# A two-block transformer on one core: another order of a mixer unit's steps on ScalarE and VectorE, squares added in twos, and the last gate's columns summed at another place

## The chip, the cores and the metric

The kernel runs on one core of one Trainium2 chip. The metric is the device time of one execution in microseconds, the median over several runs. The kernel before takes 1094.76 us (three runs, 1092.68 to 1098.1). One more execution was taken with the hardware profiler; it took 1096.54 us, of which 1094.6 us lie between its first and its last instruction (the span). All durations below are of that execution.

## The reference

A residual stream x of 256 tokens by 1024 features goes through three layers, all in float32. Each layer has a mixer (projection, attention, output projection) and a feed-forward part, and each part is normed on the way in; in the first two layers also on the way out. Scale, shift and gate of every part are a vector times a matrix. Cut to what matters:

```python
def first_block(x, c, ...):                       # two layers
    for layer in range(2):
        shift, scale, gate = split(c @ mod_w[layer, 0] + mod_b[layer, 0])
        h = rms_norm(x, norm_w[layer, 0, 0]) * (1.0 + scale) + shift
        y = mixer_ab(h, ...) if layer == 0 else mixer_cd(h, ...)
        x = x + gate * rms_norm(y, norm_w[layer, 0, 1])
        shift, scale, gate = split(c @ mod_w[layer, 1] + mod_b[layer, 1])
        h = rms_norm(x, norm_w[layer, 1, 0]) * (1.0 + scale) + shift
        y = swiglu(h, ffn_w_in[layer], ffn_w_out[layer])
        x = x + gate * rms_norm(y, norm_w[layer, 1, 1])
def mixer_cd(h, ...):    # softmax heads, and heads with stick-breaking weights
    o_c = moba_attention(...)
    o_d = stick_breaking_attention(...)
    return concatenate([o_c, o_d]) @ w_out
def second_block(x, c_2, ...):                    # one layer
    sh1, sc1, gt1, sh2, sc2, gt2 = split(silu(c_2) @ w_ada + b_ada, 6)
    h = rmsnorm(x, g_norm1) * (1.0 + sc1) + sh1
    q, k, v, z = split(h @ w_in)                  # q, k normed per head and rotated
    attn = block_attention(q, k, v)
    tok = chunked_token_mlp(z, g_tok_v, w_s, b_s)
    x = x + gt1 * (concatenate([rmsnorm(attn), rmsnorm(tok)]) @ w_out)
    h = rmsnorm(x, g_norm2) * (1.0 + sc2) + sh2
    x = x + gt2 * conv_glu_ffn(h, w_up, w_conv, b_conv, w_down)
    return rmsnorm(x, g_final)
```

## The kernel before, in words

Features lie on the 128 partitions, tokens along the free dimension. The weights come as 270 units of 128x1024 floats through a ring of six slots (`raw`, loaded by SyncE). To multiply in float32 with the fast format, each unit is split: ScalarE writes the high part `wH` (L785), VectorE the low part `wL` = raw - `wH` (L1200), and TensorE does three matmuls for each 128x128 piece: high by high, high by low, low by high (L1841 to L1843). A unit is eight pieces, so 24 matmuls; the activations are split the same way into `hH` and `hL`. An engine waits on semaphores and works strictly in the order in which its instructions are written.

The phases follow one another: the first mixer (called ab), feed-forward f0, mixer cd, feed-forward f1, mixer sb (the second block), feed-forward f2, the last norm. In a feed-forward phase a step is three units (gate, up, down).

A mixer phase cd or sb starts with projection units e = 0 to 17 (cd) or 0 to 13 (sb). For each unit, TensorE's `project` fills a bank of PSUM; ScalarE's `unit_column` copies the bank's column 256 into `ucol` (L863; it carries the shift); VectorE's `take_unit` multiplies the bank by `rstd` (L1325, L1327); ScalarE's `finish_unit` adds the column (L870; in sb the square of q and k, L1107, comes first). Beside this, ScalarE splits one later unit at the top of each pass of the loop (`split_upto(base + e + 5)`), and so does VectorE. VectorE also runs `jobs`: 128x1024 products (L602, L604) that build the columns of scale, shift and gate of later parts in `acc0`, `acc1` and `late_acc`. For the units that hold values, TensorE turns the finished unit (`turn_values`, L1920), and VectorE copies it (`values`, L1337). From unit 6 on, TensorE's project of unit e waits until VectorE has taken unit e - 2. Then come the heads, and after them eight output units (`y_unit`).

In sb some more steps lie between the units: after unit 5 ScalarE makes six activations for the norms of q and k (L1116, L1117); VectorE scales q and k at e = 7 and rotates them at e = 9 (L1745 to L1747); TensorE's first scores (`block_scores`, L2385) wait for that and for the finish of unit 10. Behind the heads TensorE sums the columns `modA5` (L1869) and turns the attention output when VectorE has scaled it (L1805, L2461).

The norms: A0 to A6 of x, B0 to B3 of a part's output y, in the order A0, B0, A1, B1, and so on; A6 is the last. ScalarE squares four blocks of 128x512 (L805), TensorE multiplies each block's two halves of 256 columns by a matrix of ones into one sum in bank 6 (L1855, L1856: eight matmuls for a norm), ScalarE makes `rstd` from it (L795, L796). VectorE waits for `rstd` and updates x (L1286, L1297), x is split again (L832, L1265), and TensorE starts the next phase. Between the sums and that start it makes a gate's columns (`mod_sum`, 8 columns) and six spare products (`keep_clock`, L1981).

At the end of f2, TensorE does down(20), then `mod_sum("modG5")` (the last gate), then down(21). VectorE takes the gate, adds the gated output to x (L1311, eight instructions) while ScalarE squares x block by block, and the last norm's eight products (L1275) end the kernel. ScalarE's split of the unit for down(21) is the last of its step, behind `aH` (L935).

## Time and profile before

| | |
|---|---|
| time, median of 3 runs | 1094.76 us |
| the profiled execution: time, span | 1096.54 us, 1094.6 us |
| TensorE (PE) busy | 1036.2 us, 95% |
| VectorE (DVE) busy | 789.8 us, 72% |
| ScalarE (ACT) busy | 557.4 us, 51% |
| mean granted TensorE clock | 0.963 of full speed |
| chain that ended last | PE 75%, DVE 11%, ACT 7%, issue 4%, DMA 3% |
| moved by DMA | 227.60 MB, mean 208 GB/s |

How to read it: busy is the time in which an engine had an instruction in work. The chain is followed back from the last instruction, at each step to what released it, so its shares tell which engine set the time at each moment. The phases in time: cd's units run from about 399 to 462 us, its heads to 502, its output units to 531; sb's units from about 746 to 812, its heads to 854, its output units from 861 on; f2 ends at about 1084. In a row of the timeline stand the start, the duration, engine, line, operation, written and read tile, shape, and in brackets the idle time before it and what ended that.

### The profile page before, as it was taken

What the parts mean: (1) busy time and instruction counts of PE and PEld (TensorE: products, weight loads), DVE (VectorE), ACT (ScalarE), POOL (GpSimd) and SP (SyncE); (2) the same over time, 40 slices, a digit from 0 to 9 for tenths busy, and PEclk for the clock granted to TensorE, in tenths of its full rate; (3) what the DMA queues carried; (4) which work ended last, traced back from release to release, by engine and by line L of the source; (5) the groups of instructions that cost most, each with busy time, mean ns of one, the idle gap of its engine ahead of it and who ended that gap; (6) DMA issues with size and microseconds to landing.
All of it is one profiled execution on the core that took longest, in us unless ns stands there. A gap on an engine that the chain in (4) does not pass through costs nothing.

```text
span 1094.6 us, 21376 instructions
## 1 busy us (share of the span) xinstructions
PE 1036.2 (95%) x8164; PEld 990.6 (90%) x8164; DVE 789.8 (72%) x1288; ACT 557.4 (51%) x1116; POOL 4.6 (0%) x14
## 2 busy tenths in 40 slices
PE   6998879999999999999999999999779999999997
PEld 5997659999999989889899999998767999999996
DVE  4757775788888757768688888765584557787775
ACT  2445663544444454454554444454551366766663
POOL 0100000000000000000000000000000000000000
PEclk9999899999999999979999999999885999999999
DMA  9966666388787647703558888753530134555441
GB/s 361 329 212 219 229 220 244 123 321 301 291 300 291 255 140 246 269 21 112 177 215 320 307 292 305 289 215 131 193 116 1 39 137 154 181 208 186 173 138 56
DMA packets 62409, 227.60 MB, mean 208 GB/s; under 512 B 7010, under 2 KB 7266, under 8 KB 61956
## 3 DMA queue, kind: packets, MB, share of 16 engines
q1 hardware_dynamic: 61556, 224.02, 57.0%
q0 software_dynamic: 640, 2.10, 0.8%
q8 instruction: 48, 0.79, 0.3%
q10 hardware_dynamic: 144, 0.52, 0.1%
q14 instruction: 21, 0.17, 0.0%
HBM read 225.04 MB, written 1.57 MB: 207 GB/s over the span
## 4 chain that ended last, share of the span: by engine, by line
PE 75%; DVE 11%; ACT 7%; issue 4%; DMA 3%; SPq 1%; DVEq 0%; ACTq 0%
PE bank L1841 20%; PE bank L1842 20%; PE bank L1843 20%; ACT wH L785 3%; DMA modbuf<-in_mod_w 3%; DVE acc L604 2%; DVE wL L1200 2%; PE bank L1856 2%; PE bank L1855 2%; PE bank L1869 1%; PE bank L2451 1%; PE bank L1950 1%; DVE otok L1286 1%; PE bank L1981 1%; PE bank L2385 1%
## 5 line engine op out<-in xcount | busy, mean ns | idle before, releaser
L1841 PE MATMUL bank<-hH,wH 128*128 128x258 f32 (+1 forms) x1544 | 448.7, 291 | 10.9 <-DVE hL L1265 7.7
L1842 PE MATMUL bank<-hL,wH 128*128 128x258 f32 (+1 forms) x1544 | 440.8, 286 | 0.0
L1843 PE MATMUL bank<-hH,wL 128*128 128x258 f32 (+1 forms) x1544 | 439.1, 284 | 0.0
L1200 DVE TENSOR_TENSOR wL<-raw,wH 128x1024 fp32r<-128x1024 f32 x270 | 328.1, 1221 | 66.6 <-ACT wH L785 66.4
L1841 PEld LDWEIGHTS bank<-hH,wH 128*128 128x128 f32 x1544 | 295.5, 191 | 20.6 <-issue 13.6
L1843 PEld LDWEIGHTS bank<-hH,wL 128*128 128x128 f32 x1544 | 296.6, 192 | 0.0
L1842 PEld LDWEIGHTS bank<-hL,wH 128*128 128x128 f32 x1544 | 296.1, 192 | 0.5
L785 ACT ACTIVATE wH<-raw 128x1024 fp32r<-128x1024 f32 x270 | 275.5, 1046 | 38.1 <-DMA raw<-in_weights 19.6
L1841 PE MATMUL bank<-aH,wH 128*128 128x256 f32 x592 | 168.6, 285 | 1.2 <-DVE wL L1200 1.2
L1843 PE MATMUL bank<-aH,wL 128*128 128x256 f32 x592 | 168.0, 284 | 0.0
L1842 PE MATMUL bank<-aL,wH 128*128 128x256 f32 x592 | 168.0, 284 | 0.0
L1841 PEld LDWEIGHTS bank<-aH,wH 128*128 128x128 f32 x592 | 113.9, 192 | 2.2 <-DVE wL L1200 1.4
L1842 PEld LDWEIGHTS bank<-aL,wH 128*128 128x128 f32 x592 | 114.0, 193 | 0.0
L1843 PEld LDWEIGHTS bank<-aH,wL 128*128 128x128 f32 x592 | 113.9, 192 | 0.0
L903 ACT ACTIVATE fcol<-bank 128x1 f32<-128x1 f32 x132 | 15.2, 166 | 136.0 <-PE bank L1843 135.9
L1414 DVE TENSOR_TENSOR sn<-bank,rstd 128x256 f32<-128x256 f32 x44 | 18.7, 424 | 51.2 <-ACT fcol L903 51.1
L935 ACT ACTIVATE aH<-sn 128x256 fp32r<-128x256 f32 x66 | 27.5, 417 | 49.4 <-PE bank L1843 24.9
L604 DVE SCALAR_TENSOR_TENSOR acc<-modbuf,par,acc 128x1024 f32<-128x1024 f32 x28 | 35.8, 1280 | 10.3 <-DMA modbuf<-in_mod_w 9.6
L1434 DVE SCALAR_TENSOR_TENSOR pr<-sq,par,pr 128x255 f32<-128x255 f32 x44 | 19.3, 481 | 29.9 <-ACT pr L921 29.9
L908 ACT ACTIVATE sn<-sn,fcol 128x256 f32<-128x256 f32 x44 | 22.4, 510 | 28.3 <-DVE sn L1414 28.3
L917 ACT ACTIVATE sq<-sq,fcol 128x256 f32<-128x256 f32 x44 | 20.1, 503 | 21.0 <-DVE sq L1425 21.0
L1286 DVE TENSOR_TENSOR otok<-bank,rstd 128x512 f32<-128x512 f32 x16 | 10.6, 685 | 25.7 <-ACT rstd L796 25.7
(324 smaller groups left out, 1212.5 us busy)
## 6 DMA issues: line engine op xcount, KB each, us to landing
raw<-in_weights SPq DMA_DIRECT2D x270, 512.0 KB, 4.5
modbuf<-in_mod_w SPq DMA_DIRECT2D x69, 512.0 KB, 6.2
modbuf<-in_w_ada SPq DMA_DIRECT2D x36, 512.0 KB, 6.3
strips<-in_mod_w SPq DMA_DIRECT2D x16, 512.0 KB, 7.2
strips<-in_w_ada SPq DMA_DIRECT2D x12, 512.0 KB, 6.7
strips<-bias_table POOLq DMA_DIRECT2D x8, 256.0 KB, 7.1
otok<-in_cmp_w SPq DMA_DIRECT2D x4, 512.0 KB, 8.4
raw<-in_mod_w SPq DMA_DIRECT2D x2, 512.0 KB, 4.7
```

The lines of the kernel that those rows point to most:

```text
L604: ops.scalar_tensor_tensor(out=dst, in0=src, scalar=cc[:, k:k + 1], in1=dst, op0=ALU.mult, op1=ALU.add).then_inc(mod_used, 1)
L785: nc.scalar.activation(wH[:, slot, :], raw[:, slot, :], ACT.Copy).then_inc(hi_ready[c], 1)
L908: nc.scalar.activation(sn[:, t % 2, 0:S], sn[:, t % 2, 0:S], ACT.Silu, bias=fcol[:, t % 2, 0:1]).then_inc(silu_ready, 1)
L917: last = nc.scalar.activation(z, z, ACT.Identity, bias=fcol[:, t % 2, n:n + 1])
L935: nc.scalar.activation(aH[:, t % 2, :], sn[:, t % 2, S:2 * S], ACT.Copy).then_inc(aH_ready, 1)
L1200: V.tensor_tensor(wL[:, slot, :], raw[:, slot, :], wH[:, slot, :].bitcast(F32), ALU.subtract).then_inc(lo_ready[c], 1)
L1286: chain.inc(V.tensor_tensor(tt[:, 2 * b:2 * b + 2, :], bank[(2 if i == 0 else 0) + b][:, :].rearrange("p (k s) -> p k s", k=2), bcast(rstd ...
L1841: mm(out, lhs_h, rhs_h, start=start, stop=False, skip_group_check=True)
L1842: mm(out, lhs_h, rhs_l, start=False, stop=False, skip_group_check=True)
L1843: return mm(out, lhs_l, rhs_h, start=False, stop=stop, skip_group_check=True)
L1855: mm(bank[6][:, 0:S], ones, buf[:, 0:S], start=(b == 0), stop=False, skip_group_check=True)
L1856: mm(bank[6][:, 0:S], ones, buf[:, S:2 * S], start=False, stop=(b == 3), skip_group_check=True).then_inc(sq_used, 1)
```

## The change

Three edits. First, in both mixers a unit's split moves. ScalarE issues it between `unit_column` and the waits ahead of `finish_unit`, VectorE after `take_unit`; each unit is split in the pass before the one that split it until now, behind that pass's copy of the column. The number of splits stays 270.

On ScalarE in cd, three units in a row. `ucol` is the column, `proj` the unit's tile, `wH` the split. Before:

```order
L785 ACTIVATE wH<-raw 128x1024 [waits unit_used0,raw_full3]
L863 ACTIVATE ucol<-bank 128x1 [waits unit_used2]
L870 ACTIVATE proj<-proj,ucol 128x256 [waits unit_scaled,ucol_ready]
L785 ACTIVATE wH<-raw 128x1024 [waits unit_used1,raw_full4]
L863 ACTIVATE ucol<-bank 128x1 [waits unit_used0]
L870 ACTIVATE proj<-proj,ucol 128x256 [waits unit_scaled,ucol_ready]
```

The same place now:

```order
L874 ACTIVATE proj<-proj,ucol 128x256 [waits unit_scaled,ucol_ready]
L866 ACTIVATE ucol<-bank 128x1 [waits unit_used2]
L788 ACTIVATE wH<-raw 128x1024 [waits unit_used1,raw_full4]
L874 ACTIVATE proj<-proj,ucol 128x256 [waits unit_scaled,ucol_ready]
L866 ACTIVATE ucol<-bank 128x1 [waits unit_used0]
L788 ACTIVATE wH<-raw 128x1024 [waits unit_used2,raw_full5]
```

The split stood behind the finish of a unit, and stands ahead of it now.

On VectorE at the end of cd's units (unit 17, then the first stick-breaking head, L1660 and L1671). `vt` are the values, `strips` a job. Before:

```order
L1200 TENSOR_TENSOR wL<-raw,wH 128x1024 [waits hi_ready0]
L1325 TENSOR_TENSOR sq<-bank,rstd 128x256 [waits v_turned,ucol_ready]
L1337 COPY vt<-bank 128x2x128 [waits v_turned]
L604 SCALAR_TENSOR_TENSOR strips<-modbuf,csil,strips 128x1024 [waits mod_used,job_full2]
L1337 COPY vt<-bank 128x2x128 [waits v_turned,con_landed]
L1660 TENSOR_TENSOR sq<-bank,con 128x384 [waits z_psum]
```

And now:

```order
L1336 TENSOR_TENSOR sq<-bank,rstd 128x256 [waits v_turned,ucol_ready]
L1202 TENSOR_TENSOR wL<-raw,wH 128x1024 [waits hi_ready1]
L1348 COPY vt<-bank 128x2x128 [waits v_turned]
L607 SCALAR_TENSOR_TENSOR strips<-modbuf,csil,strips 128x1024 [waits mod_used,job_full2]
L1348 COPY vt<-bank 128x2x128 [waits v_turned,con_landed]
L1671 TENSOR_TENSOR sq<-bank,con 128x384 [waits z_psum]
```

A further unit's low part stands between taking unit 17 and the first head; it stood behind the last head. In sb it is the same with unit 13.

Second, for the norms B0, B1, B2, B3 and A6 VectorE adds the two halves of each block of squares in place (`add_pair`, four for a norm), and TensorE makes one matmul for a block instead of two. On TensorE, the sums of norm A6 before:

```order
L1855 MATMUL bank<-sq,con 128x256 [waits sq_ready,rstd_ready]
L1856 MATMUL bank<-sq,con 128x256
L1855 MATMUL bank<-sq,con 128x256 [waits sq_ready]
L1856 MATMUL bank<-sq,con 128x256
L1855 MATMUL bank<-pr,con 128x256 [waits sq_ready]
L1856 MATMUL bank<-pr,con 128x256
L1855 MATMUL bank<-pr,con 128x256 [waits sq_ready]
L1856 MATMUL bank<-pr,con 128x256
```

These eight rows are now three, of which the last stands for two matmuls:

```order
L1889 MATMUL bank<-con,strips 128x128 [waits mod_used]
L1889 MATMUL bank<-con,strips 128x128 x7
...
L1870 MATMUL bank<-sq,con 128x256 [waits pair_ready,rstd_ready]
L1870 MATMUL bank<-sq,con 128x256 [waits pair_ready]
L1870 MATMUL bank<-pr,con 128x256 [waits pair_ready] x2
```

The two rows of L1889 ahead of them are the third edit: the eight columns of the last gate, `mod_sum("modG5")`, stand much earlier in TensorE's row, right behind `mod_sum("modA5")` of sb, and write bank 6; they stood between down(20) and down(21) of f2. VectorE takes them with `modA5`'s.

```diff
+        PAIRED = [1, 3, 5, 7, 10]
         def mod_bank(name):
-            return bank[6 if name == "modA1" else 7]
+            return bank[6 if name in ("modA1", "modG5") else 7]
...
+        NUNITS = {"cd": CD_UNITS, "sb": SB_UNITS}
...
                 nc.scalar.activation(ucol[:, e % 2:e % 2 + 1], proj_bank(phase, e)[:, S:S + 1], ACT.Copy,
                                      scale=scale).then_inc(ucol_ready, 1)
+                split_upto(min(BASE[phase] + e + 6, BASE[phase] + NUNITS[phase] + 5))
                 act.wait_ge(ucol_ready, SCALED0[phase] + e + 1)
                 act.wait_ge(unit_scaled, SCALED0[phase] + e + 1)
...
             for e in range(18):
-                split_upto(min(base + e + 5, end + 5))
                 if e == 17:
...
+            def add_pair(n, b):
+
+                buf = squares_buffer(n, b)
+                dve.wait_ge(sq_ready, 4 * n + b + 1)
+                V.tensor_tensor(buf[:, 0:S], buf[:, 0:S], buf[:, S:2 * S], ALU.add).then_inc(pair_ready, 1)
+
             def norm_b(i, m, a, late, base):
 
-                dve.wait_ge(rstd_ready, NORMS.index(f"B{i}") + 1)
+                n = NORMS.index(f"B{i}")
+                for b in range(4):
+                    add_pair(n, b)
+                dve.wait_ge(rstd_ready, n + 1)
...
             for e in range(18):
-                split_upto(min(base + e + 5, end + 5))
                 if e == 16:
                     neg_scores(24, 0)
                 take_unit("cd", e, CD_SCALE[e])
+                split_upto(min(base + e + 6, end + 5))
                 values("cd", e)
                 jobs_upto(cd_jobs(e))
...
-                split_upto(min(base + e + 5, end + 5))
                 take_unit("sb", e)
+                split_upto(min(base + e + 6, end + 5))
                 values("sb", e)
...
             mod_take("modA5")
+            mod_take("modG5")
...
             ffn("f2", 5)
-            mod_take("modG5")
             for b in range(4):
                 residual("f2", 5, b)
+                if b >= 1:
+                    add_pair(NORMS.index("A6"), b - 1)
+            add_pair(NORMS.index("A6"), 3)
             norm_a(6)
...
-                pe.wait_ge(sq_ready, 4 * n + b + 1)
                 buf = squares_buffer(n, b)
+                if n in PAIRED:
+                    pe.wait_ge(pair_ready, 4 * PAIRED.index(n) + b + 1)
+                    mm(bank[6][:, 0:S], ones, buf[:, 0:S], start=(b == 0), stop=(b == 3),
+                       skip_group_check=True).then_inc(sq_used, 1)
+                    return
+                pe.wait_ge(sq_ready, 4 * n + b + 1)
...
-                mod_sum({"f0": "modA2", "f1": "modA4", "f2": "modG5"}[phase])
+                if phase != "f2":
+                    mod_sum({"f0": "modA2", "f1": "modA4"}[phase])
                 down(FT - 1)
...
             mod_sum("modA5")
+            mod_sum("modG5")
             pe.wait_ge(an_out, 2)
```

## Rows read from the trace of the kernel before

**Rows 1.** Waits of TensorE: line, waited for, us in total, times, longest.

```profile
PE bank L1920 <- ACT sq L870: 6.3, 3, 4.4
PE bank L2451 <- DVE pt L1356: 2.8, 1, 2.8
PE bank L2385 <- ACT proj L870: 2.4, 1, 2.4
```

**Rows 2.** Timeline of ScalarE at norm B0: the last two squares.

```profile
183.40 1.33 ACT L805 ACTIVATE pr<-bank 128x512 f32<-128x512 f32 x2
```

**Rows 3.** Timeline of TensorE at norm B0: first and last sum, next phase.

```profile
183.94 0.59 PE L1855 MATMUL bank<-sq,con 128*128 128x256 f32 x2
...
186.96 0.59 PE L1856 MATMUL bank<-pr,con 128*128 128x256 f32 x2
...
192.25 0.36 PE L1841 MATMUL bank<-hH,wH 128*128 128x258 f32 x1 [1.57 <-DVE hL L1265]
```

**Rows 4.** Groups by line: a 128x256 operation of VectorE; busy, mean ns.

```profile
L1454 DVE TENSOR_TENSOR aL<-sn,aH 128x256 fp32r<-128x256 f32 x66 | 27.7, 419 | 1.0 <-ACT aH L935 1.0
```

**Rows 5.** Timeline of ScalarE in cd: one unit, and unit 17's column.

```profile
418.49 1.04 ACT L785 ACTIVATE wH<-raw 128x1024 fp32r<-128x1024 f32 x1
...
421.22 0.51 ACT L870 ACTIVATE proj<-proj,ucol 128x256 f32<-128x256 f32 x1 [1.63 <-DVE proj L1325]
421.63 1.04 ACT L785 ACTIVATE wH<-raw 128x1024 fp32r<-128x1024 f32 x1
...
461.78 0.17 ACT L863 ACTIVATE ucol<-bank 128x1 f32<-128x1 f32 x1
```

**Rows 6.** Timeline of VectorE in cd: a split, and the first head.

```profile
419.56 1.22 DVE L1200 TENSOR_TENSOR wL<-raw,wH 128x1024 fp32r<-128x1024 f32 x1 [0.39 <-ACT wH L785]
...
464.48 0.55 DVE L1660 TENSOR_TENSOR sq<-bank,con 128x384 f32<-128x384 f32 x1
```

**Rows 7.** Timeline of TensorE in cd: two matmuls of unit 2, units 6 and 15.

```profile
409.02 0.28 PE L1842 MATMUL bank<-hL,wH 128*128 128x258 f32 x1
409.14 0.28 PE L1843 MATMUL bank<-hH,wL 128*128 128x258 f32 x1
...
421.18 0.39 PE L1841 MATMUL bank<-hH,wH 128*128 128x258 f32 x1 [0.60 <-DVE proj L1325]
...
450.10 0.44 PE L1920 MATMUL bank<-con,sq 128*128 128x128 f32 x2 [0.57 <-ACT sq L870]
```

**Rows 8.** Busy by stretch, cd's heads, sb's unit 12, sb's heads: engines, then PEclk.

```profile
466.50:480.10 13.60, 13.55 (x53) 11.50 (x53) 8.06 (x24) 5.69 (x16) 0.00 (x0) 0.50 0.01 4
...
801.00:808.00 7.00, 6.80 (x27) 6.00 (x28) 5.95 (x8) 2.51 (x5) 0.00 (x0) 0.51 0.60 184
...
818.20:852.80 34.60, 34.52 (x137) 26.87 (x138) 16.52 (x30) 6.14 (x25) 0.00 (x0) 0.51 0.01 1
```

**Rows 9.** Timeline of ScalarE in sb: after the norms of q and k, unit 6.

```profile
776.87 1.04 ACT L785 ACTIVATE wH<-raw 128x1024 fp32r<-128x1024 f32 x1
...
779.58 1.28 ACT L870 ACT_TABLE_LOAD   x1 [1.61 <-DVE sq L1325]
780.87 0.51 ACT L870 ACTIVATE sq<-sq,ucol 128x256 f32<-128x256 f32 x1
```

**Rows 10.** Timeline of TensorE behind sb's heads.

```profile
854.31 5.58 PE L1869 MATMUL bank<-con,acc 128*128 128x128 f32 x48
860.96 1.10 PE L2461 MATMUL bank<-con,otok 128*128 128x128 f32 x8 [1.07 <-DVE otok L1805]
```

**Rows 11.** Timeline of TensorE at the end of f2.

```profile
1078.07 1.95 PE L1869 MATMUL bank<-con,strips 128*128 128x128 f32 x16
1081.20 0.39 PE L1841 MATMUL bank<-aH,wH 128*128 128x256 f32 x1 [1.17 <-DVE wL L1200]
...
1087.19 0.59 PE L1856 MATMUL bank<-pr,con 128*128 128x256 f32 x2
```

**Rows 12.** Timeline of ScalarE at the end: the last square.

```profile
1085.54 0.63 ACT L805 ACTIVATE pr<-x 128x512 f32<-128x512 f32 x1
```

9 lines of the change are left out of this document (5 added, 4 removed).

## The prediction

> **What bounds the kernel now.** I read in this order: busy shares, TensorE's waits, then the timelines of three engines wherever TensorE stands still. TensorE is busy 95% of the span, so a gain has to come from fewer TensorE instructions on the path, from its idle time, or from stretches at the lower clock. The reader is to see four places.
>
> At norm B0 TensorE runs eight sums without a break; the last of them starts at 186.96, although ScalarE's last square had ended at 183.40 + 1.33 = 184.73 [rows 2, 3]. ScalarE and VectorE wait for these sums, and TensorE waits for them in turn: its next phase starts at 192.25 after 1.57 us idle [rows 3]. The eight matmuls are the path.
>
> In cd a ring bounds the units. ScalarE starts a high part at 418.49, VectorE its low part at 419.56 (1.14 us at its own pace), takes the unit behind it, ScalarE finishes that unit at 421.22 and starts the next high part at 421.63 [rows 5, 6]. That is 3.14 us for a unit. TensorE's matmuls start 0.12 us apart, so a unit of 24 needs 2.89 [rows 7]. TensorE falls behind by 0.25 a unit.
>
> In sb the waits are few and long: 4.4 us for the finish of unit 6, 2.4 for that of unit 10, 2.8 for VectorE's first copy of probabilities [rows 1]. Behind the last two the granted clock is 0.51, the 1.2 GHz level; in cd's heads it is 0.50 for 13.6 us, in sb's heads 0.51 for 34.6 us [rows 8]. Behind idle times of 1.57, 1.17 and 1.07 us matmuls go on at the 2.4 GHz level [rows 3, 10, 11].
>
> At the end of f2 down(21) starts at 1081.20, released by VectorE's low part and not by TensorE's own gate columns, which had started at 1078.07 [rows 11].
>
> **The change, part by part.**
>
> *Norms B0 to B3.* Removed: four matmuls of (186.96 - 183.94) / 7 = 0.43 us each [rows 3]. Added: four additions of 256 columns on VectorE, which waits there anyway. The trace has no such addition; the nearest row is a 128x256 subtraction of two SBUF tiles, 0.42 us [rows 4]. Below, 0.34 (the pace at which such operations follow each other); above, 0.7 (one of 512 columns). I take 0.42. Three additions are hidden behind the squares. The last is not: the square ends at 184.73, a hand-over costs 0.05 to 0.1, the addition ends at 185.2, and the last matmul starts at 185.25 instead of 186.96: 1.7 gained. B1 and B3 run the same; in B2 the last square comes from an output unit's end instead of a queue of squares, which makes it 1.65. TensorE's gate columns and spare products still end before it is wanted. Sum: 6.8 us (at 0.7 for an addition: 5.7).
>
> The Trainium skill (VectorE: DVE Perf Modes, The TRN2 errata) says that an operation reading SBUF pays a fixed cost per instruction on VectorE and none on TensorE, and advises tiles of 512 elements or more; four additions of 256 go against that. The row agrees, 0.42 us for 256 columns, so the exchange is 0.42 for 0.43 and gains only where a queue of sums stands in front. That is so in B0 to B3 and not in A6, below.
>
> *The ring in cd.* ScalarE now issues the high part while VectorE takes the unit. For each unit ScalarE has 0.15 + 1.04 + 0.41 = 1.6 us, VectorE 0.34 + 1.14 + two thirds of a job of 1.2, and 0.34 for a value: 2.3 to 2.6. Both are under 2.89, and the units stay split five ahead, so TensorE is the bound. From unit 6 to the turning ahead of unit 15 it took 450.10 - 421.18 = 28.9 us, where nine units need 26.0, and before unit 6 it lost 0.76 (0.60 idle and the rest of the gap) [rows 7]: 3.7 gained when unit 17 ends. Then something is given back. VectorE's order there is take, low part, copy, job, copy, first head. The low part waits for a high part begun just before: it starts about 1.2 us behind the column and ends at 2.35, so the first head starts 4.3 us behind unit 17's column instead of 464.48 - 461.78 = 2.7 [rows 5, 6]. Late by 1.6. Behind the heads that split goes, but the output units there are bound by TensorE. Net: 2.1 gained.
>
> *The ring in sb.* Walking the same steps: until unit 6 the ring (0.4 longer, for the square) costs TensorE 1.5. Unit 5's finish then comes 3.4 earlier, the six norm activations (3.3 us) follow it, and for unit 6 the path from their end to the finish falls from 780.87 - 776.87 = 4.0 to 0.15 + 1.04 + 1.28 = 2.5, as the table load no longer waits behind low part and take [rows 9]. TensorE's 4.4 idle becomes 1.1 and unit 8 starts 5.0 earlier. Behind 1.1 us idle the clock should hold, so unit 8 runs in 2.9 and not at half speed: another 2.4, together 7.4. The rotations at e = 9 now wait for a low part: idle before the first scores 3.0 instead of 2.4, and 7.1 remain; unit 12 stays at the lower level. Behind unit 13 VectorE has low part and two jobs ahead of the first copy, with the wait for the high part: 1.5 lost. Net: 5.6 gained at the heads. These run at half speed with TensorE never idle [rows 8], and keep it.
>
> The Trainium skill (ScalarE: Activation LUTs, What ACT_TABLE_LOAD costs) gives a table switch 1.28 us and about as much again for draining, 2.66 in all. Here the activation starts 780.87 - 779.58 = 1.29 behind the load [rows 9], so the measurement decides. By the page, TensorE's idle time would be 2.5 us, unit 8 slow again, and the time some 3.7 higher.
>
> *The gate's columns.* In sb they add 16 instructions behind the 48, (1081.20 - 1.17) - 1078.07 = 1.8 us with their tail [rows 11]. Before, TensorE stood 1.07 there, waiting for VectorE [rows 10]. So 0.75 is lost. In f2 they were hidden: down(21) still waits for its split until 1081.20, and nothing is gained. But TensorE is now idle from 1078.2 on, 3.0 us instead of 1.17. The shortest idle time behind which a row shows the lower clock is 2.4, the longest behind which it held 1.57. I take it that it falls. Then 24 matmuls take 0.22 to 0.24 each, and the last block of y comes 2.5 later.
>
> *Norm A6.* VectorE adds between its updates of x: block 3's update moves by 0.7, its square from 1085.54 to 1086.3 [rows 12], then come an addition and one matmul, at 1087.5 instead of 1087.19 [rows 11]. So 0.3 is lost at full clock. With the lower clock all of it is behind the last y: 2.4 together.
>
> Sum: 6.8 + 2.1 + 5.6 - 0.75 - 2.4 = 11.35 us. From the profiled execution's 1096.54 this gives 1085.2; the median of the runs, 1094.76, is 1.8 below that execution, so 1083.4.
>
> **The rivals.**
>
> 1. The clock holds at the end of f2. For: nothing shows where between 1.57 and 2.4 us it is decided, and whether a phase matters. Against: 3.0 is longer than two idle times that cost it. It gives back 2.1: 1081.3.
>
> 2. Transfers bind. In cd, 2/3 of a job and one unit, 0.87 MB, must land every 2.89 us: 302 GB/s, against some 270 there before. If 270 is the limit the pitch is 3.24 and the 3.7 are gone; ScalarE would wait for `raw`, and hold the finish too. For: ScalarE's split now stands ahead of the finish. Against: f0 and f1 move 300 GB/s and more by the page's slices, and six slots are a long lead. 1087.1.
>
> 3. The lower clock stays longer in cd's heads. TensorE's idle ahead of the second head grows from 1.2 to 2.9 us, since the first head is 1.6 later. It was low for 13.6 us and TensorE recovered under way [rows 8]. A head takes 6.6 us then and 3.65 at full clock. One further stretch of half that length costs 3.0: 1086.4. The slower side is the same mechanism to its end: the clock does not recover, as it did not in sb's heads for 34.6 us [rows 8]. Six heads, 2.9 more each, cost 17: 1100.8. It decides if no recovery comes before the last head. Against: the same matmuls brought it back at 480.
>
> 4. sb's gain is swallowed by VectorE's queue, at the rotations and at the first copy, so that only 2 of 5.6 remain: 1087. For: VectorE is the engine waited for there. Against: no instruction is added, and most of the gain is made before.
>
> 5. sb's heads get full clock for a part, because the idle time ahead of them falls differently. Each three heads at full speed would bring 6: about 1077. Against: their idle time grows to some 4.9 us.
>
> **How the numbers follow.** Forecast 0.55; rival 1 0.14; rival 2 0.07; rival 3 with 1086.4 0.10, with 1100.8 0.04; rival 4 0.06; rival 5 0.04. A nearly equal pitch and the norms' gain alone, near 1089, is left as no case of its own. The range takes rivals 1 to 4 but the slow end, and the additions at 0.7: 1079 to 1090. No change is within 0.5%, about 5.5 us, which is what a measurement can tell: above 1089.3 lie parts of rivals 2 and 4. Faster 0.91, same 0.05, slower 0.04.
>
> **What would show it.** Right, if four sums of 0.43 stand at each B norm with the last start 1.7 earlier; if units 6 to 14 of cd follow at 2.9 us; if the idle time ahead of sb's unit 8 is near 1 us at full clock, and the first copy of probabilities comes 5.6 earlier measured from sb's first unit; if down(21) starts at the same distance behind down(20), with PEclk near 0.5. The forecast is wrong if ScalarE waits for `raw` in cd, if cd's heads start earlier by less than 1 us against its first unit, or if PEclk stays at 0.50 through cd's heads.

## The result, and the profile after

The changed kernel takes 1077.78 us (median of four runs, 1077.3 to 1083.13) against 1094.76. The ratio over all runs is 0.9853, 95% interval 0.9813 to 0.9893; that of the medians is 0.9845. It is faster by 17.0 us where 11.35 were forecast, and 1.2 us below the low end of the range. The same kernel, run four more times beside nine runs of the kernel before, gave 1081.13 (1078.52 to 1082.12) against 1095.2, a ratio of 0.9876 (0.9857 to 0.9896). Of all eight runs the median is 1079.56, of the 64 runs of the kernel before beside the experiments 1095.03: 15.5 us. The first four runs were thus some 2 us on the lucky side, and the forecast was still short by 4.

Some lines of the page of the changed kernel: busy time with share and instructions, TensorE's clock in 40 slices, the chain that ended last.

```profile
span 1075.5 us, 21315 instructions
PE 1016.7 (95%) x8124; PEld 974.8 (91%) x8124; DVE 797.9 (74%) x1308; ACT 558.5 (52%) x1116; POOL 4.6 (0%) x14
...
PEclk9999999999999999989999999999975999999998
...
PE 82%; DVE 9%; ACT 4%; issue 2%; DMA 2%; SPq 1%; DVEq 0%; ACTq 0%
```

TensorE's busy time fell by 19.5 us, the span by 19.1. The idle time that went was replaced by idle time elsewhere, and what fell is the length of matmuls: 20 of them are gone, and more run at the 2.4 GHz level. The table follows the lead of the changed kernel through the two profiled executions. It is read from TensorE's timeline: when an instruction starts before, when the same one starts now. The table's first line is no gain of the change: in a second profile of the changed kernel the sums of B0 start at 184.52, later than before.

| from ... to | gained here, us | forecast |
|---|---|---|
| start to the sums of B0 (183.94, 182.50): nothing changed here | 1.4 | 0 |
| norms B0, B1, B2, B3 | 1.6, 1.6, 1.5, 1.6 | 1.7, 1.7, 1.65, 1.7 |
| cd's units (turn of unit 17: 461.58, 453.05) | 3.85 | 3.7 |
| second head's products (465.68, 458.60) | -1.45 | -1.6 |
| **cd's heads, to their end (501.95, 490.37)** | **4.5** | **0** |
| sb: unit 6, unit 8, unit 9, first scores, each counted from sb's start | 1.4, 5.2, 7.5, 6.9 | 1.5, 5.0, 7.4, 7.1 |
| **sb: first sums of values (818.28, 796.59)** | **7.0** | **5.6** |
| sb's heads, gate's columns | -0.6, -0.55 | 0, -0.75 |
| end of f2 and last norm | -1.45 | -2.4 |

The ends of cd's heads, by TensorE's timeline of the kernel before and of the changed one (the gate columns that follow the heads):

```profile
501.95 3.79 PE L1869 MATMUL bank<-con,acc 128*128 128x128 f32 x32
```

```profile
490.37 3.79 PE L1889 MATMUL bank<-con,acc 128*128 128x128 f32 x32
```

At norm B0 four sums stand where eight stood [rows 3]. TensorE's timeline of the changed kernel:

```profile
182.50 1.02 PE L1870 MATMUL bank<-sq,con 128*128 128x256 f32 x4
183.36 1.14 PE L1870 MATMUL bank<-pr,con 128*128 128x256 f32 x4
184.34 1.95 PE L1889 MATMUL bank<-con,acc 128*128 128x128 f32 x16
...
189.20 0.36 PE L1855 MATMUL bank<-hH,wH 128*128 128x258 f32 x1 [1.57 <-DVE hL L1267]
```

From the first sum to the next phase it is 6.7 us instead of 8.3, with the same 1.57 us of idle time. The additions, by VectorE's groups of lines, took 0.42 us, the value taken from [rows 4]:

```profile
L1286 DVE TENSOR_TENSOR pr<-pr 128x256 f32<-128x256 f32 x10 | 4.2, 423 | 2.3 <-ACT pr L808 2.1
```

TensorE's waits (us in total, times, longest), against [rows 1]:

```profile
PE bank L2472 <- DVE pt L1367: 4.6, 1, 4.6
PE bank L1855 <- DVE wL L1202: 4.3, 2, 3.0
PE bank L2406 <- ACT proj L874: 3.0, 1, 3.0
PE bank L2328 <- DVE otok L1674: 2.5, 1, 2.5
PE bank L1940 <- ACT sq L874: 2.3, 2, 1.4
```

The 4.4 us ahead of sb's unit 8 are gone. In their place the waits that the forecast had named are longer: ahead of cd's second head 2.5 instead of 1.2, the first scores 3.0 instead of 2.4, the first sums of values 4.6 instead of 2.8, down(21) 3.0 instead of 1.2.

Why the second head waits stands on VectorE, which answers to [rows 6]: unit 17's take, the low part, copy, job, copy, and only then the head.

```profile
453.45 0.42 DVE L1336 TENSOR_TENSOR sq<-bank,rstd 128x256 f32<-128x256 f32 x1 [1.65 <-ACT ucol L866]
454.40 1.23 DVE L1202 TENSOR_TENSOR wL<-raw,wH 128x1024 fp32r<-128x1024 f32 x1 [0.53 <-ACT wH L788]
...
457.41 0.55 DVE L1671 TENSOR_TENSOR sq<-bank,con 128x384 f32<-128x384 f32 x1
```

Now the clock. Busy time by stretch, with the granted clock as the third number from the end, of cd's heads, of the end of f2 and of sb's heads in the changed kernel, against [rows 8]:

```profile
455.60:458.60 3.00, 0.51 (x3) 0.11 (x1) 2.91 (x6) 0.02 (x1) 0.00 (x0) 0.63 0.58 190
458.60:463.20 4.60, 4.60 (x15) 3.78 (x16) 2.52 (x8) 3.13 (x8) 0.00 (x0) 0.50 0.38 119
463.20:484.00 20.80, 20.80 (x159) 19.05 (x159) 18.49 (x54) 13.23 (x37) 0.00 (x0) 1.00 0.01 2
...
796.59:833.26 36.67, 36.67 (x148) 28.73 (x149) 16.43 (x29) 6.73 (x26) 0.00 (x0) 0.52 0.00 1
...
1062.00:1068.50 6.50, 5.65 (x28) 4.14 (x27) 4.74 (x12) 2.52 (x4) 0.00 (x0) 0.85 0.00 0
```

In cd's heads the 1.2 GHz level ends at 463.2 and had lasted 6.8 us, part of it while TensorE stood still; before it lasted 13.7. That is the 4.5 us of the table. sb's heads stay at that level for 37.5 us; in the two profiles of the kernel before it is 34.1 and 40.9. At the end of f2 it lasts 3.4 us, 15 of the 24 last products.

### The profile page after: what moved, and what is told of

The parts are those of the page before. It is cut to its first block, busy times and chain, and to the rows that moved or that the text cites. A ratio compares the mean times of both kernels' runs of the same rounds, so it can differ in the third digit from the quotient of the medians.

```text
span 1075.5 us, 21315 instructions
## 1 busy us (share of the span) xinstructions
PE 1016.7 (95%) x8124; PEld 974.8 (91%) x8124; DVE 797.9 (74%) x1308; ACT 558.5 (52%) x1116; POOL 4.6 (0%) x14
## 3 DMA queue, kind: packets, MB, share of 16 engines
HBM read 225.04 MB, written 1.57 MB: 211 GB/s over the span
## 4 chain that ended last, share of the span: by engine, by line
PE 82%; DVE 9%; ACT 4%; issue 2%; DMA 2%; SPq 1%; DVEq 0%; ACTq 0%
PE bank L1855 22%; PE bank L1856 22%; PE bank L1857 22%; DVE acc L607 2%; PE bank L1889 2%; DMA modbuf<-in_mod_w 1%; PE bank L2472 1%; ACT wH L788 1%; DVE wL L1202 1%; PE bank L1970 1%; DVE otok L1297 1%; PE bank L1875 1%; PE bank L1874 1%; PE bank L1870 1%; DMA otok<-in_cmp_w 1%
## 5 line engine op out<-in xcount | busy, mean ns | idle before, releaser
L1855 PEld LDWEIGHTS bank<-hH,wH 128*128 128x128 f32 x1544 | 292.4, 189 | 17.5 <-issue 13.0
L1856 PEld LDWEIGHTS bank<-hL,wH 128*128 128x128 f32 x1544 | 293.1, 190 | 0.5
L907 ACT ACTIVATE fcol<-bank 128x1 f32<-128x1 f32 x132 | 15.2, 166 | 136.3 <-PE bank L1857 136.1
L607 DVE SCALAR_TENSOR_TENSOR acc<-modbuf,par,acc 128x1024 f32<-128x1024 f32 x28 | 35.9, 1281 | 10.2 <-DMA modbuf<-in_mod_w 9.1
L835 ACT ACTIVATE hH<-x,sc 128x256 fp32r<-128x256 f32 x40 | 18.2, 503 | 22.3 <-DVE x L1308 14.5
```

What stands on the lines that cost most here:

```text
L607: ops.scalar_tensor_tensor(out=dst, in0=src, scalar=cc[:, k:k + 1], in1=dst, op0=ALU.mult, op1=ALU.add).then_inc(mod_used, 1)
L1855: mm(out, lhs_h, rhs_h, start=start, stop=False, skip_group_check=True)
L1856: mm(out, lhs_h, rhs_l, start=False, stop=False, skip_group_check=True)
```

## The experiments

Sixteen kernels, and both originals once more, bear on five questions. Each was run four to twelve times in turns with the kernel before; times are medians, with the lowest and highest in brackets. "Low time" is the time at the 1.2 GHz level, added up from the granted clock of stretches of 1 us. Spare products are matmuls of TensorE on constants whose result nobody reads.

### Which edit is worth what

Each of the three edits alone, and the change without the third. As a diff against the changed kernel, the first is

```diff
-                split_upto(min(BASE[phase] + e + 6, BASE[phase] + NUNITS[phase] + 5))   # and VectorE's likewise
+                split_upto(min(base + e + 5, end + 5))                                  # at the loop's top again
-            mod_sum("modG5")                                                            # back to the end of f2
```

the second `PAIRED = []` with the additions left out and the gate's columns back, the third both of these without the last line.

> The kernel before with the additions in twos alone (norms B0 to B3 and A6). Theory 1 (the terms stand by themselves, and what was missed is the clock in cd's heads): 1.6 us from each B norm, 6.4 in all, A6 costs up to 0.3; the lower clock in cd's heads lasts about as long as before, 13.6 us; about 1088.5 us. Theory 2 (every edit that moves cd's heads to another moment changes how long the clock stays low there, whatever the edit is): the same 6.4, and the stretch at PEclk 0.50 in cd's heads differs from 13.6 us by several us.

Measured: 1089.3 (1085.9 to 1091.5), ratio 0.995 (0.9935 to 0.9964): 5.75 gained.

> The kernel before with the moved splits alone, in cd and sb. Theory 1: cd's units 3.8 us shorter, 1.5 given back at the first head, the idle time ahead of cd's second head grows from 1.2 to 2.9 us, the clock falls in it, and the low stretch that costs is about 4.6 us instead of 13.6: 4.5 more gained; sb 7 us; together about 13.5 to 14: near 1081. Theory 2: the same without the 4.5, which came with the moment and not with the idle time: near 1085.5.

Measured: 1082.4 (1081.3 to 1084.6), ratio 0.988 (0.9865 to 0.9895): 12.6 gained where the forecast has 7.7. This is the term that was mis-sized.

> The kernel before with the last gate's columns moved behind modA5, nothing else. My theory: 0.6 us lost behind sb's heads, nothing gained at the end, where TensorE is idle for 3.0 us ahead of down(21), the clock falls in it and costs about 1.5 to 2: 1096.5 to 1097.5. Rival (the clock holds at the end, or the gate was on the path): 1094 to 1095.4, PEclk 1.0 in down(21).

Measured: 1097.25, ratio 1.0017 (1.0006 to 1.0028): 2.2 lost, against 2.85. From sb's last columns to the turn it takes 7.20 us instead of 6.65, and the rest is lost at the end, where the clock falls behind 2.96 us of idle time (TensorE's timeline, then busy time by stretch, of this kernel):

```profile
1081.64 0.55 PE L1851 MATMUL bank<-aH,wH 128*128 128x256 f32 x1 [2.96 <-DVE wL L1203]
```

```profile
1080.00:1084.50 4.50, 2.86 (x13) 2.86 (x14) 2.10 (x3) 1.84 (x3) 0.00 (x0) 0.69 0.00 0
```

> The changed kernel with the gate's columns back between down(20) and down(21). My theory: TensorE's idle time there is 1.2 us again and the clock holds, the last sums come about 1.5 to 2 us earlier, and 0.6 us come back behind sb's heads: some 2 us faster than the changed kernel, near 1076. Rival (the gate's place is worth nothing): 1077 to 1078.5.

Measured: 1078.8 (1074.2 to 1081.5), ratio 0.9856. No fall at the end of f2, and in its profile 1.0 us less from the turn to the end and 0.55 less ahead of it; between the medians nothing of this can be told.

The new order was then tried in one mixer at a time (`if phase == "cd":`, `if phase == "sb":` in front of the split in `unit_column`, the other phase's loops as before).

> The kernel before with the new order in cd alone (no paired sums, sb's order and the gate's columns as before). The forecast's term: 3.7 gained at unit 17, 1.6 given back, net 2.1, and no change in the heads: median 1093. Theory (the term missed time at the lower clock in the heads): net 2.1 to 2.5 from the order, and 0 to 4.5 more by how long the clock stays low in the heads of each execution: median 1090 to 1093, and the stretch from the second head's products to the end of the heads takes 30.9 us with no low clock, 31.3 with 3.4 us of it, 31.8 with 6.8, 34.3 with 10.2 and 36.3 with 13.7.

> The kernel before with the new order in sb alone (no paired sums, cd's order and the gate's columns as before). The forecast's term: 7.1 gained at the first scores, 1.5 given back ahead of the first sums of values, net 5.6: median 1089.4. Theory (nothing is given back there, since the wait for the first copy ends in the shadow of the slower second scores): 7.0 gained at the first sums of values and at the end, median 1088. Rival (the sb part of the change moved the clock of cd's heads too, or holds more than its own place): cd's heads change although cd's order is before's, median under 1086.

Measured: cd alone 1090.0 (1087.3 to 1091.8), ratio 0.9948 (0.9932 to 0.9963), sb alone 1088.1 (1086.7 to 1092.4), ratio 0.9944 (0.9927 to 0.9961), beside 1094.9 for the kernel before: 4.9 and 6.8 gained. In the profile of cd alone the heads run low for 10.2 us; in that of sb alone the first scores start 6.9 sooner and the first sums of values 7.05, counted from sb's start. In that profile the low time in cd's heads is 10.2 us and the heads are about 2 us shorter, though nothing in cd is changed, so the 6.8 may hold some of it. Added up, 5.75 + 4.9 + 6.8 - 2.2 = 15.3, near the 15.5 of all runs; each term is known to 1.2 to 1.9 us, so that they meet so closely is luck. The forecast has 6.5 + 2.1 + 5.6 - 2.85 = 11.35.

### Is it the clock in cd's heads?

Spare products in the two idle times ahead of the heads, in the changed kernel and in the kernel before:

```diff
+            keep_clock(bank[6], 4)
             turn_values("cd", 18)
...
                     scores(24 + s, s, 0, 4)
+                    if s == 1:
+                        keep_clock(bank[6], 8)      # 3 in the kernel before
                     stick_z(s)
```

> The changed kernel with 4 spare products on TensorE ahead of the turn of cd's last values and 8 behind the second head's scores, in the two idle times ahead of the stick-breaking heads (1.40 and 2.49 us in the changed kernel's trace). They use nothing and change no result. Theory 1 (what the forecast missed in cd is time at 1.2 GHz in the heads: 13.7 us of it before, 6.8 us in the changed kernel's profiled run): with shorter idle times the clock holds, the granted clock of the stretch behind the turn reads 1.00, the heads from the turn to their end take about 34 us instead of the 37.3 us of the changed kernel, and the median is 0.5 to 3 us below 1077.8, about 1076. Rival (the heads are bound by VectorE's and ScalarE's work and the clock there costs nothing; the 4.5 us came from order): the heads take 37.3 us whatever the clock, the median stays at 1077.8 within 0.5 us or rises by the spare products.

> The kernel before, with nothing of the change, and spare products on TensorE ahead of cd's heads: 4 ahead of the turn of the last values (idle 1.27 us there), 3 behind the second head's scores (idle 1.16 us). Theory (the forecast's missing 4.5 us in cd are time at the 1.2 GHz level, which the order of ScalarE's and VectorE's steps does not cause by itself): without any of the change the heads run at 1.00, the stretch from the second head's products to the end of the heads shortens from 36.3 us (13.7 us of it low) to 30.9 us, as measured in the changed kernel with spare products, and the median falls from 1095 to 1090 or 1092. Rival (the changed order itself shortens the heads): the stretch stays 34 us or more though the clock reads 1.00, and the median stays within 1 us of before's.

> The kernel before with the new order in cd alone and with spare products ahead of cd's heads (4 and 8). It stands to the kernel before with spare products alone (1091.45 us) as the order in cd does where the clock is held. Theory (the order is worth 3.85 - 1.45 = 2.4 us, the rest was clock): 1089.0, and the heads take 30.9 us from the second head's products. Rival (the order shortens the heads by itself, 4.9 us in all as in the run without spare products): 1086.5.

Measured: 1078.6 (1076.3 to 1080.3) for the changed kernel with them; 1091.45 (1089.0 to 1094.2), ratio 0.997 (0.9957 to 0.9982), for the kernel before; 1088.75 (1087.2 to 1089.3) for the new order in cd. In all three the clock holds. Busy time by stretch of the kernel before with spare products, its heads:

```profile
466.50:480.00 13.50, 12.81 (x91) 11.13 (x92) 11.23 (x34) 9.45 (x26) 0.00 (x0) 1.00 0.08 31
480.00:497.00 17.00, 16.81 (x128) 15.39 (x127) 12.98 (x34) 9.75 (x27) 0.00 (x0) 1.00 0.01 1
```

and of the new order in cd with them:

```profile
463.80:494.70 30.90, 30.01 (x220) 26.91 (x221) 24.60 (x68) 19.20 (x52) 0.00 (x0) 1.00 0.06 19
```

All profiles of this case together tell what the lower level costs there. The stretch is from the second head's products to the heads' end:

| low time in cd's heads, us | the stretch takes, us | profiles |
|---|---|---|
| 0 | 30.9 | six, four of the new order, two of the old |
| 3.4 | 31.3 | six |
| 6.8 | 31.8 | the changed kernel |
| 10.2 | 34.3 to 34.5 | four |
| 13.7 | 36.3 to 36.6 | three, the kernel before twice |

The order makes no difference to the heads: 30.9 us with both, once the clock is the same. The first 6.8 us at the lower level cost only 0.9 (part of them falls on the idle time ahead of the stretch, as the granted clock of 0.63 there shows), and each further 3.4 us cost 2 to 2.7. In medians the spare products bring 3.4 us to the old order, 1.3 to the new one in cd (1090.0 to 1088.75), and 1.0 to the changed kernel (1079.6 to 1078.6). So the order is worth 2.7 where the clock is held (1091.45 to 1088.75; 3.0 if each is set against the kernel before in its own series, 1094.9 and 1095.2), near the forecast's 2.1, and 4.9 where it is not. These differences are of the size of their intervals, some 2 us; the lengths of the heads in the table are the firmer evidence.

Does the low time belong to the kernel or to the execution? Both kernels were profiled again.

> The kernel before once more, for a second profile. Theory (time at the lower clock in cd's heads differs between kernels more than between executions, since spare products there brought 3.4 us to this kernel's order and 1.3 to the new one): median 1095, 10.2 or 13.7 us low in the heads. Rival (the 13.7 us were that execution's): 0 to 6.8 us low, and the end of the heads 2 to 5 us nearer to their start.

> The changed kernel once more, for a second profile and more times. Theory (the low time in cd's heads varies from execution to execution, 3.4 to 10.2 us): median 1077.8 within 1 us. Rival (it belongs to the kernel): 6.8 us again.

Measured: the kernel before 1095.8 beside itself at 1094.3 (ratio 1.0005, 0.9984 to 1.0026), with 13.7 us low in the heads as in the first profile; the changed kernel 1081.1, with 3.4 us instead of 6.8. Busy time by stretch of the kernel before in its second profile, the heads:

```profile
465.60:479.40 13.80, 13.35 (x53) 11.32 (x54) 7.38 (x22) 6.26 (x16) 0.00 (x0) 0.56 0.07 28
```

In these two pairs of profiles it repeats within one step of 3.4 us, which speaks against mere chance. Yet it isn't the order of cd alone either: with the paired norms alone, where nothing in cd is changed and the idle times ahead of the heads are nearly those of before (1.22 and 1.03 us), the profile shows 3.4 us. That profile was of the fastest of six runs, by 2.4 us, and the median of those runs shows no such gain. Nor is it the length of the idle time: the kernel before stays low for 13.7 us behind 1.27 and 1.16 us, the changed one for 3.4 or 6.8 behind 1.40 and 2.49.

Of the 14 profiles without spare products in cd, the seven that have the paired norms and no late split (a variant described below) show 3.4 us, once 6.8, and the other seven 10.2 or 13.7, whichever order cd has. No run tests whether the paired norms do this, and the median of the paired norms alone speaks against it. What decides between 3.4 and 13.7 stays open.

### What starts the long stretch in sb's heads?

```diff
                     if e == 12:
+                        keep_clock(bank[7], 8)
                         pe.wait_ge(qk_done, 3)
...
+                if s == 2:
+                    keep_clock(bank[2], 14)
                 if s >= 2:
                     h = s - 2
```

> The changed kernel with 8 spare products on TensorE ahead of sb's first scores (idle 2.97 us there) and 14 ahead of the first sums of values (idle 4.63 us). Theory 1 (the idle time ahead of them starts the long stretch at 1.2 GHz, 37.6 us in the changed kernel's trace, and with the heads' own matmuls TensorE does not win the full clock back): if the spare products hold the clock, the stretch from the first sums of values to the gate columns shortens from 36.7 us by up to half of it, and the median falls by 5 to 15 us, to about 1068. Rival (what TensorE does in the heads sets the clock and not the idle time ahead of them): the clock falls some us later at the latest, the stretch stays 33 to 37 us, and the median moves by less than 2 us, to 1076 to 1078.

> The changed kernel with 14 spare products on TensorE ahead of the first sums of values alone; the idle time of 2.97 us ahead of the first scores stays. Theory (the long stretch at the lower clock starts with the idle time of 4.63 us ahead of the sums of values, and the short one behind the first scores ends by itself among units 12 and 13): the heads run at 1.00, median 1062 to 1063.5. Rival (both idle times act together, as the clock has just come back at 785): the heads stay low, median 1078 to 1080.

Measured: with both, 1062.0 (1061.2 to 1062.9 in five runs, 1077.8 in the sixth), ratio 0.9695 (0.9673 to 0.9717). With the second alone, 1065.9, 1066.9 and 1066.9 in three runs and 1076.9, 1078.1 and 1079.7 in three. TensorE's timeline of the kernel with both:

```profile
776.22 1.95 PE L2001 MATMUL bank<-con 128*128 128x128 f32 x16
779.41 0.67 PE L2406 MATMUL bank<-proj 64*128 64x256 f32 x2 [1.24 <-ACT proj L874]
...
792.67 3.29 PE L2001 MATMUL bank<-con 128*128 128x128 f32 x28
796.41 1.10 PE L2475 MATMUL bank<-vt,pt 128*128 128x64 f32 x8 [0.45 <-DVE pt L1367]
```

The second group fills 4.63 us of idle time down to 0.45, and the heads behind it take 21.4 us at full clock where they took 36.7. By stretch:

```profile
796.40:817.80 21.40, 20.47 (x148) 16.56 (x149) 15.54 (x29) 6.70 (x26) 0.00 (x0) 1.00 0.01 2
```

With the second group alone, the profiled execution was one in which the clock fell, though only 1.51 us of idle time were left:

```profile
796.84 1.23 PE L2474 MATMUL bank<-vt,pt 128*128 128x64 f32 x8 [1.51 <-DVE pt L1367]
```

```profile
800.00:833.00 33.00, 33.00 (x137) 25.95 (x137) 13.16 (x24) 5.70 (x22) 0.00 (x0) 0.52 0.01 1
```

So these heads don't have to be slow. In all 20 profiles they keep, to their end or nearly, the level that they have 1 us behind their start: TensorE is busy all the time at half speed and still stays there, and it stands idle for 1 us of 21 at full speed and keeps that. Neither theory was right for the second group alone: by the times of the six runs (mean granted clock 0.979 to 0.983 in the fast three, 0.966 to 0.969 in the others), 1.5 us of idle time kept or lost the clock by the execution. With both groups it held in five runs of six here, and in all 15 runs of three more kernels below, by their times.

### The change with the clock held

> The kernel before, with nothing of the change, and spare products ahead of cd's heads (4 and 3), of sb's first scores (6) and of the first sums of values (8). Theory (sb's heads stay at the 1.2 GHz level only because an idle time ahead of them brought it down): they run at 1.00 for some 21.4 us instead of 36.0, median 1091.45 - 15 = 1076. Rival (the long low stretch ends only in the changed kernel, where the idle time is cut in another way): 1090 to 1091.

> The changed kernel with spare products ahead of cd's heads (4 and 8), sb's first scores (8) and first sums of values (14), and the last down products of f2 (8). Theory (with the clock held the change is worth its order alone: norms 6.5, cd 2.4, sb 7.0, gate's columns -0.5, end 0): 15.4 us below the kernel before with spare products, and 1 to 2 us below the changed kernel with spare products in sb alone (1062.0): about 1060.5. Rival (the change's gain was mostly clock): the difference between the two kernels with spare products is under 12 us.

The diffs are those above, in both kernels (in the kernel before 4, 3, 6 and 8 spare products), and 8 more ahead of down(21) in the changed one. Measured: 1075.0 (1074.6 to 1076.8), ratio 0.9819 (0.9802 to 0.9837), for the kernel before; 1060.6 (1059.5 to 1062.4), ratio 0.9689 (0.9672 to 0.9706), for the changed one. Both spread less than most sets without spare products. Their difference is the change with the clock held in the heads of cd and sb: 14.45 us, known to some 2.7, where the terms expected 15.4 and the rival under 12. It isn't free of the clock altogether: in the kernel before, TensorE is still low for 6.9 us behind the 4.4 us of idle time ahead of sb's unit 8, and its eight spare products ahead of the first sums of values are more than the wait holds and delay them by 0.5. The heads of sb in the kernel before with spare products, by stretch:

```profile
817.00:834.50 17.50, 16.96 (x125) 13.55 (x125) 11.81 (x23) 5.67 (x22) 0.00 (x0) 1.00 0.01 1
```

The kernel before thus gains 20 us from 21 spare products, more than from the whole change.

The Trainium skill (TensorE: Matmul & The Clock Gate, Part 1, "What's actually happening") puts the loss from the clock's ramp at a kernel's start at under 1% of a typical kernel's span and says that the number of slow matmuls changes from run to run. The time that spare products won here is lost in the middle of the kernel, not at its start, and is 1.8% (1095.2 to 1075.0), so that figure can't stand for it. That the slow part changes from run to run this case shows too: 6.8 and 3.4 us in cd's heads in two profiles of the changed kernel.

### Two edits to what is given back

> The changed kernel with 8 spare products on TensorE ahead of the last tile's down products at the end of f2 (idle 2.95 us there, behind which the clock falls to 1.2 GHz for some 3.4 us, and again at the end). Theory (the fall costs the end 1.5 us): granted clock 1.00 through these products, the end comes 1 to 1.7 us sooner after the wait, median about 1076.3. Rival (the wait on VectorE sets the end and the last products are hidden, or the spare products push the last ones back): median 1077.8 within 0.5 us.

Measured: 1079.7 (1076.2 to 1081.5). The clock holds, 1.00 through the last products of f2, and in the profile the end comes 13.7 us behind down(21)'s start instead of 14.85. The medians can't tell it from nothing, among runs that spread over 5 us.

> The changed kernel in which, on ScalarE and VectorE, the last unit of cd and the last unit of sb split no weights ahead: these two splits stand behind the units' columns as in the kernel before. Theory (the forecast's terms of +1.6 us at the end of cd's units and of some 1.5 us in sb, given back because the last split stands ahead of the last columns): the second head's products come 1.4 us sooner in cd and the first scores or sums of values 1 to 1.5 us sooner in sb, median 1075 (1074 to 1076.5). Rival (those waits end by another chain, the work is only moved and the next weights come later by as much): median 1077.8 within 1 us.

```diff
-                split_upto(min(BASE[phase] + e + 6, BASE[phase] + NUNITS[phase] + 5))
+                if not ((phase == "cd" and e == 17) or (phase == "sb" and e == 13)):
+                    split_upto(min(BASE[phase] + e + 6, BASE[phase] + NUNITS[phase] + 5))
```

Measured: 1077.0 (1074.5 to 1081.5), ratio 0.9839 (0.9813 to 0.9865). In the profile the second head follows the first spare products of B1 by 65.7 us instead of 67.4, so 1.8 came back; but the heads were low for 10.2 us in that execution and took 34.25, which ate it. These 10.2 us came behind idle times of 1.11 and 1.02 us, shorter than those of the changed kernel: a shorter idle time alone did not hold the clock. The wait ahead of the first sums of values fell from 4.6 to 3.2, but the low time behind the first scores was 6.9 us instead of 3.4. The medians leave 0.8 to 2.6 us, less than they can tell.

All of it together, without the gate's edit:

> The changed kernel without the gate's edit (its columns stay in f2), with the last splits of cd and sb behind the units' columns, with spare products ahead of cd's heads (4 and 4) and of sb's first scores (8) and first sums of values (10). Theory (late splits gain 1.4 us in each phase once the clock holds, the spare products keep cd's and sb's heads at 1.00, the gate's columns beside f2's wait hold the clock at the end): from the 1062.0 us of the changed kernel with spare products in sb alone, 1 to 1.5 less in cd, 0 to 1 less in sb, 0.5 less in cd's heads, 1 less at the end: about 1059. Rival (ten spare products are too few where fourteen held, and the clock falls in sb's heads): 1076.

Measured: 1056.7 (1055.4 to 1059.3), ratio 0.9661 (0.9647 to 0.9675), the fastest version of this case: 38 us below the kernel before and 21 below the changed one. It was expected at 1059; with the clock held behind the first scores, the late split brings the first sums of values 15.2 us behind them instead of 16.9, more than the 0 to 1 us expected in sb. Ten spare products held the clock in sb as fourteen had. Busy time by stretch, from the first scores to the first sums of values and sb's heads:

```profile
776.00:791.00 15.00, 12.91 (x88) 11.00 (x88) 13.21 (x17) 9.61 (x22) 0.00 (x0) 1.00 0.43 140
791.50:812.90 21.40, 20.44 (x148) 16.53 (x149) 15.57 (x29) 6.68 (x26) 0.00 (x0) 1.00 0.01 2
```

## Why the forecast was wrong, step by step

- **Norms B0 to B3:** right. 6.3 against 6.8 in the profile, with four sums of 0.43 and additions of 0.42; 5.75 in the median with A6 in it, against 6.5.
- **The ring in cd:** right to the start of the heads. 3.85 gained at unit 17 and 1.45 given back, against 3.7 and 1.6. Wrong from there, and this is the main step that failed: "Behind the heads that split goes, but the output units there are bound by TensorE. Net: 2.1 gained." That took the heads' time as fixed. It was not: 36.3 us with 13.7 low, 31.8 with 6.8 low. The step priced the lower clock as part of the heads' length, and the rivals had it last longer (rival 3) or end sooner in sb (rival 5), but none had it end sooner in cd. In medians this is 2.8 of the 4 us that were missed (4.9 against 2.1), and some 2 of it go when the clock is held. The forecast also counted 2.4 us as the shortest idle time behind which a row shows the lower clock. In cd's heads of the kernel before, low from 466.5 on, it had fallen behind 1.27 and 1.16 (TensorE's timeline):

```profile
463.24 0.44 PE L1920 MATMUL bank<-con,sq 128*128 128x128 f32 x2 [1.27 <-ACT sq L870]
...
465.68 0.70 PE L2307 MATMUL bank<-proj 64*128 64x256 f32 x2 [1.16 <-DVE otok L1663]
```

- **The ring in sb:** the walk through units 6, 8 and 9 came out within 0.2 us, with 0.91 us of idle time ahead of unit 8 and the clock at full speed behind it. (From 7.4, a wait longer by 0.6 leaves 6.8 at the first scores, where the forecast wrote 7.1 and the trace shows 6.9.) What failed is the step "Behind unit 13 VectorE has low part and two jobs ahead of the first copy, with the wait for the high part: 1.5 lost": from the first scores to the first sums of values nothing was lost, and 7.0 were left instead of 5.6. TensorE's timeline, the first scores, the second scores and the first sums of values, of the kernel before in its first profile, in its second, and of the changed kernel:

```profile
801.20 1.19 PE L2385 MATMUL bank<-proj 64*128 64x256 f32 x2 [2.41 <-ACT proj L870]
...
808.31 0.70 PE L2385 MATMUL bank<-proj 64*128 64x256 f32 x2
...
818.28 1.97 PE L2451 MATMUL bank<-vt,pt 128*128 128x64 f32 x8 [2.75 <-DVE pt L1356]
```

```profile
800.18 0.67 PE L2385 MATMUL bank<-proj 64*128 64x256 f32 x2 [2.41 <-ACT proj L870]
...
805.80 0.70 PE L2385 MATMUL bank<-proj 64*128 64x256 f32 x2
...
817.27 1.97 PE L2451 MATMUL bank<-vt,pt 128*128 128x64 f32 x8 [0.89 <-DVE pt L1356]
```

```profile
779.65 0.67 PE L2406 MATMUL bank<-proj 64*128 64x256 f32 x2 [2.97 <-ACT proj L874]
...
785.25 0.70 PE L2406 MATMUL bank<-proj 64*128 64x256 f32 x2
...
796.59 1.97 PE L2472 MATMUL bank<-vt,pt 128*128 128x64 f32 x8 [4.63 <-DVE pt L1367]
```

The sums follow the first scores by 17.1, 17.1 and 16.9 us. The clock is not the reason: in the second profile of the kernel before TensorE was low for 3.4 us behind the first scores instead of 6.8, the second scores came 1.5 sooner, and the sums no sooner. They wait for VectorE's first copy of probabilities (VectorE's timeline, taking unit 13 and that copy, before and after):

```profile
814.62 0.42 DVE L1325 TENSOR_TENSOR proj<-bank,rstd 128x256 f32<-128x256 f32 x1 [2.40 <-ACT ucol L863]
...
817.54 0.68 DVE L1356 COPY pt<-bank 128x512 f32<-128x512 f32 x1
```

```profile
791.18 0.42 DVE L1336 TENSOR_TENSOR proj<-bank,rstd 128x256 f32<-128x256 f32 x1 [1.59 <-ACT ucol L866]
...
795.85 0.68 DVE L1367 COPY pt<-bank 128x512 f32<-128x512 f32 x1
```

From the take to the copy it is 4.67 us instead of 2.92, so the loss that was forecast came, 1.75. But the take itself follows the first scores by 11.5 us instead of 13.4, because ScalarE, with one split less in the way, begins the first head's probabilities (with their table load) 7.6 us behind the first scores instead of 9.7. The forecast left out this gain of 1.9.
- **The table load:** the finish of unit 6 started 1.28 us behind it again, and no 1.4 more followed. ScalarE's timeline, against [rows 9]:

```profile
758.79 1.05 ACT L788 ACTIVATE wH<-raw 128x1024 fp32r<-128x1024 f32 x1
759.85 1.28 ACT L874 ACT_TABLE_LOAD   x1
761.15 0.51 ACT L874 ACTIVATE sq<-sq,ucol 128x256 f32<-128x256 f32 x1
```

- **The gate's columns and A6:** right in kind. The lower clock came behind the idle time of 2.95 us, as assumed, but it lasted for 15 of the 24 products: 1.45 lost at the end against 2.4. In sb it is 0.55 against 0.75: the columns took 1.62 us more and 1.07 of idle time went. (The difference that the forecast wrote down for them, (1081.20 - 1.17) - 1078.07, is 1.96 and not 1.8.) A6's last matmul starts 7.25 us behind down(21)'s start at this clock, where the eight sums were done 6.0 behind it before.
- **Rivals:** 1 fell (the clock did not hold behind 2.95 us), 2 fell (nothing was lost to `raw` in cd, where the 3.85 us came; the slices of f0 that the forecast read as 300 GB/s and more are 255 to 321), 3 had the place right and the sign wrong, 4 fell, and 5 named 1077, the time that came, by a mechanism that did not: sb's heads stayed low for 37.5 us. That its number fits is chance.
- **The scale:** the forecast went from a profiled execution to the median by one difference, -1.8 us. Runs of one kernel spread over 5 to 7 us here, and the first four runs of the changed kernel were 1.8 below its median of eight. So some 1.5 of the 5.65 us between forecast and result are luck of the runs (17.0 against 15.5).

Shown: what each edit is worth within 1.2 to 1.9 us, that cd's heads take the same time in either order at one clock, that spare products in the idle time ahead of heads keep the clock up, and that the missing 1.4 us in sb are not clock. Not shown: why the kernel before stays low for 13.7 us in cd's heads and the changed one for 3.4 to 6.8, and whether it is the spare products' work or the shorter idle time that holds the clock.

## What to carry to other kernels

Where a stretch of a profile runs at the lower clock, price it as a term of its own, in both directions: what it costs is read from the same stretch at the other level, and its length can differ between kernels and executions in which the stretch itself is the same. Look for the idle time ahead of such a stretch before anything else; a few spare products there were worth more than three careful edits. And a wait that grows is no loss by itself: count from the work ahead of it. Profile an unchanged kernel twice before giving a difference a cause: here the second profile of the kernel before shows that the low time behind sb's first scores cost nothing.

## What was not expected of the hardware

- sb's heads keep the level that they have just behind their start: 36.7 us at 0.52 with TensorE busy throughout, 21.4 us at 1.00 with TensorE idle for 0.9 of them (16 and 4 profiles). cd's heads come back by themselves, after 3.4 to 13.7 us.
- The same program kept the clock in three runs and lost it in three behind the same wait (1065.9 to 1066.9 against 1076.9 to 1079.7, granted clock 0.979 to 0.983 against 0.966 to 0.969). One median hides this: 1071.9 was never measured.
- The length of one idle time does not tell whether the clock falls. It fell behind 1.27 and 1.16 us ahead of cd's heads, and held behind 1.57 us at the norms in every profile and behind 2.40 ahead of sb's first scores in two (of the kernel before and of the new order in cd, both with spare products ahead of cd's heads).
- With the clock held in the heads, runs of a kernel lie within 2 to 4 us of each other (1074.6 to 1076.8; 1059.5 to 1062.4; 1055.4 to 1059.3, five runs each); without, within 3 to 7 (1091.3 to 1098.7 over 64 runs of the kernel before).
